# First two layers' down product as block products with fewer multiplications: five of eight pieces, weight sums on GpSimd, and four smaller edits

## The reference, cut to what matters

```python
# hybrid layer, l = 0 and 1
ada = cond_act @ w_ada + b_ada                      # 6 x 1024, also for the two layers of the second block
x = layer_norm(ALPHA * x + g1 * mixed) * ln1_g + ln1_b
u2 = layer_norm(x) * (1 + sc2) + sh2
hdn = jnp.square(jax.nn.relu(u2 @ w_up + b_up))     # 256 x 4096
x = layer_norm(ALPHA * x + g2 * (hdn @ w_down)) * ln2_g + ln2_b   # w_down 4096 x 1024

# attention layer of the second block
x1, x2 = jnp.split(x, 2, axis=-1)                   # rotary: halves of each head of 64
return x * cos + jnp.concatenate([-x2, x1], -1) * sin
# softmax of q.k for 8 difference maps and 8 window heads, over own and context keys
```

## Time and profile before

| | us |
|---|---|
| median of 3 runs | 2385.49 (2384.83 to 2390.07) |
| the profiled execution, its own time | 2385.63 |
| its span, first to last instruction | 2383.8 |
| PE busy in it | 2275.2 |
| DVE busy | 1006.3 |
| ACT busy | 346.3 |
| POOL busy | 69.9 |
| granted TensorE clock, mean | 0.994 |

### The profile page before, as it was taken

The page is one execution under the profiler, slowest core; times in us unless marked ns, Lnnn a source line. Parts: engine busy times, 40 slices in busy tenths (PEclk is TensorE's granted clock), DMA queues, the critical chain, the costliest instruction groups (busy, mean ns, idle before and its releaser), DMA issues.

```text
span 2383.8 us, 26007 instructions
## 1 busy us (share of the span) xinstructions
PE 2275.2 (95%) x10472; PEld 1384.4 (58%) x10472; DVE 1006.3 (42%) x2156; ACT 346.3 (15%) x705; POOL 69.9 (3%) x100
## 2 busy tenths in 40 slices
PE   6999999999999999999999999988899999998888
PEld 4888688448888786467554444333397544443333
DVE  4265656667656567213853211111235522211112
ACT  1221011001221110011441111111100011111111
POOL 0100000002000000000000000000030000000000
PEclk9999999999999999999999999999999999999999
DMA  9745967855377688542069999999964399999997
GB/s 325 254 165 195 342 235 285 323 212 212 126 280 262 238 317 312 198 147 75 35 252 356 423 420 424 423 423 422 410 234 159 121 367 422 423 423 424 421 422 295
DMA packets 184613, 703.44 MB, mean 295 GB/s; under 512 B 9648, under 2 KB 19120, under 8 KB 159152
## 3 DMA queue, kind: packets, MB, share of 16 engines
q1 hardware_dynamic: 180688, 691.76, 74.6%
q0 software_dynamic: 3808, 10.00, 1.3%
HBM read 696.45 MB, written 5.28 MB: 294 GB/s over the span
## 4 chain that ended last, share of the span: by engine, by line
PE 77%; SPq 11%; DMA 6%; DVE 3%; ACT 1%; issue 1%; DVEq 0%; ACTq 0%
PE banks L630 75%; DMA ring<-in_exp_w_up_dram 6%; SPq L2651 4%; SPq L2653 3%; SPq L2699 2%; SPq L2649 1%; DMA ring<-in_w_ada_dram 1%; DVE arena L2239 1%; PE banks L692 0%; DVE acc L1830 0%; PE banks L1211 0%; PE banks L1019 0%; DVE acc L1803 0%; ACT UT L1463 0%; PE banks L1106 0%
## 5 line engine op out<-in xcount | busy, mean ns | idle before, releaser
L630 PE MATMUL banks<-ring,arena 128*64 128x512 f32 (+2 forms) x2624 | 719.8, 589 | 32.5 <-DMA ring<-in_exp_w_up_dram 21.1
L630 PE MATMUL banks<-UT,ring 128*128 128x256 f32 (+1 forms) x3680 | 720.5, 355 | 8.5 <-ACT UT L1463 3.9
L630 PEld LDWEIGHTS banks<-UT,ring 128*128 128x128 f32 x3680 | 619.7, 192 | 82.7 <-issue 9.5
L630 PEld LDWEIGHTS banks<-ring,arena 128*64 128x64 f32 (+1 forms) x2624 | 288.5, 151 | 433.1 <-issue 390.9
L630 PE MATMUL banks<-arena 128*64 128x512 f32 (+5 forms) x1220 | 238.8, 493 | 9.1 <-DMA arena<-in_exp_w_up_dram 4.6
L2238 DVE TENSOR_TENSOR arena<-arena,banks 128x512 f32<-128x512 f32 x32 | 34.0, 1063 | 434.6 <-PE banks L630 434.6
L1830 DVE SCALAR_TENSOR_TENSOR acc<-ring,cact,acc 128x512 f32<-128x512 f32 x280 | 212.7, 760 | 9.9
L630 PEld LDWEIGHTS banks<-arena 128*64 128x64 f32 (+2 forms) x1220 | 99.3, 158 | 135.7 <-issue 120.7
L1627 ACT ACTIVATE arena<-banks 128x512 f32<-128x512 f32 (+1 forms) x96 | 65.3, 680 | 771.4 <-PE banks L630 732.2
L2246 DVE TENSOR_TENSOR arena<-banks,acc 128x512 f32<-128x512 f32 x32 | 22.1, 692 | 185.7 <-PE banks L630 185.7
L630 PE MATMUL banks<-ring,XN 128*128 128x512 f32 (+1 forms) x192 | 73.1, 540 | 2.8 <-DVE XN L2003 2.8
(11 more groups left out here) (268 smaller groups left out, 1707.0 us busy)
## 6 DMA issues: line engine op xcount, KB each, us to landing
ring<-in_exp_w_up_dram SPq DMA_DIRECT2D x40, 2048.0 KB, 25.2
ring<-in_exp_w_gate_dram SPq DMA_DIRECT2D x40, 2048.0 KB, 26.0
ring<-in_exp_w_down_dram SPq DMA_DIRECT2D x38, 2048.0 KB, 26.2
ring<-in_w_in_dram SPq DMA_DIRECT2D x26, 2048.0 KB, 13.7
ring<-in_mod_w_dram SPq DMA_DIRECT2D x24, 2048.0 KB, 9.0
ring<-in_w_ada_dram SPq DMA_DIRECT2D x20, 2048.0 KB, 8.1
ring<-in_w_up_dram SPq DMA_DIRECT2D x16, 2048.0 KB, 9.1
ring<-in_w_down_dram SPq DMA_DIRECT2D x16, 2048.0 KB, 9.0
```

The costliest lines, as they stand in the source:

```text
L630: return nc.tensor.matmul(o, lhs, rhs, start=start, stop=stop)
```

## The change

Five parts.

1. **Down product of pieces 0 to 4**, both layers: the 2x2 blocks (two tiles of tokens by two halves of the rows; two halves of the rows by two halves of the columns) are multiplied by Winograd's form of Strassen's scheme, seven block products of two matmuls each. VectorE forms the sums of hidden blocks (`hidden_sums`, four per piece), GpSimd those of weight blocks (`down_weight_sums`, four of 128x1024), into scratch of two sets. Products 1, 5, 6, 7 stay in banks of their own over the five pieces; VectorE combines them with the gate and adds them to the residual (`shared_products`) under pieces 5 to 7. Products 2, 3, 4 and pieces 5 to 7 are summed in banks as before. The norm rows are loaded behind piece 4.
2. **Folds** in pairs: one product of 32 columns for two modulation steps, one eviction of eight columns.
3. **Swaps**: the halves of the heads are swapped by ACT, four copies of 32 partitions, from the bank into `acc`; `perm2` and its products go; the rotations of the last two query groups move into the loop, behind pairs 2 and 4.
4. **Early scores**: the first pair's scores, maxima and exponents come between the last two query groups, behind `hidsum_ready`; the lambda product moves ahead of the query pieces.
5. The gate row's store and load are separate functions, with a weight set between them.

The diff, cut to its core:

```diff
@@ tensor: modulation
+            def modulation(until, turning=False, hold=None):
+                while summed[0] + 2 <= until:
+                    n = summed[0]
+                    names = [("ada",) + MOD_STEPS[n + i] for i in range(2)]
+                    bank = take(pe, names[0], None if turning else n // 2 % 2 if hold is None else hold)
+                    group_of[names[1]] = group_of[names[0]]
+                    pe.wait_ge(acc_ready, n + 2)
+                    finish(mm(bank[:, 0:32], C("fold"), folded[:, n // 2 % 2, :, :], True, True), names[0])
+                    summed[0] = n + 2
@@ tensor: block_one
+                down = {i: take(pe, part[i]) for i in (1, 5, 6, 2, 3, 4)}
                 pe.wait_ge(hid_ready, 16 * (l + 1))
+                def strassen_piece(j):
...
+                    product(1, upper(0), w[:, 0:2, 0:512])
+                    product(2, lower(0), w[:, 2:4, 0:512])
+                    pe.wait_ge(row_sums_ready, DOWN_BOTH * l + j + 1)
+                    product(3, s4, w[:, 2:4, 512:D])
+                    pe.wait_ge(weight_sums_ready, DOWN_BOTH * l + j + 1)
+                    product(5, s1, t1)
+                    product(6, s2, t2)
+                    if j == 0:
+                        down[7] = take(pe, part[7], 0)
+                    product(7, upper(1), w[:, 0:2, 512:D])
+                    product(4, lower(1), t4).then_inc(dn_read, 1)
...
                 for j in range(DOWN_BOTH):
-                    down_piece(j, (0, 1))
-                    beside("dn", l, j)
+                    strassen_piece(j)
+                    beside("dn", l, j, hold=1)
                 for j in range(DOWN_BOTH, 8):
                     down_piece(j, (0,))
+                down[5] = take(pe, names[3])
@@ tensor: attention_block (rope_pair and its four calls removed)
                 for j in range(2):
                     w = wview(("ain", 0, j))
                     for q in range(2):
                         pair_feature(("ain", j, q, 0), w, q * N, UT)
+                        if (j, q) == (1, 0):
+                            pe.wait_ge(hidsum_ready, 1)
+                            scores(two[0])
@@ scalar
+            def swap_halves(n, bank, width, scale=1.0):
+                if n >= 2:
+                    act.wait_ge(rope_ready, 4 + n - 1)
+                for b in range(4):
+                    there, here = slice(32 * b, 32 * b + 32), slice(32 * (b ^ 1), 32 * (b ^ 1) + 32)
+                    x = A(acc[there, n % 2, 0:width], bank[here, 0:width], ACT.Copy, scale=scale)
+                x.then_inc(halves_swapped, 1)
@@ vector
+            def hidden_sums(l, j):
+                if j >= 2:
+                    dve.wait_ge(dn_read, 7 * l + j - 1)
...
+                link(V.tensor_tensor(s1, a21, a22, ALU.add))
+                link(V.tensor_tensor(s2, s1, a11, ALU.subtract))
+                V.tensor_tensor(a21, a11, a21, ALU.subtract)
+                V.tensor_tensor(s4, a12, s2, ALU.subtract).then_inc(row_sums_ready, 1)
@@ vector: block_one
                     if i % 2:
                         beside("up", l, i // 2, flush="last" if i == 15 else None)
+                dve.wait_ge(hid_ready, 16 * (l + 1))
+                for j in range(2):
+                    hidden_sums(l, j)
                 wait_evicted(dve, ("ada", l, 11, "x"))
                 gate_turn(l, 1)
                 for j in range(6):
                     beside("dn", l, j, flush="last" if (l, j) == (1, 3) else None)
+                    if j + 2 < DOWN_BOTH:
+                        hidden_sums(l, j + 2)
+                    if j == DOWN_BOTH - 1:
+                        shared_products(l)
@@ vector: attention_block, in the loop over pairs
+                    if p in (2, 4):
+                        q = p // 2 - 1
+                        wait_evicted(dve, ("ain", 1, q, 0))
+                        rotate_swapped(5 + q, QK[:, 4 + 2 * q:6 + 2 * q, :])
@@ gpsimd
+            def down_weight_sums(l, j):
+                w = piece(pool, ("dn", l, j)).rearrange("p (k d) -> p k d", d=D)
+                if j == 0:
+                    pool.wait_ge(x_ready, 4 * l + 2)
+                if j == 1:
+                    filled(pool, ("up", l, 7, 1))
+                if j >= 2:
+                    pool.wait_ge(dn_read, 7 * l + j - 1)
...
+                link(G.tensor_tensor(t1, b12, b11, ALU.subtract))
+                link(G.tensor_tensor(t2, b22, t1, ALU.subtract))
+                G.tensor_tensor(t4, b21, t2, ALU.subtract)
+                G.tensor_tensor(b12, b22, b12, ALU.subtract).then_inc(weight_sums_ready, 1)
```

214 lines of the change are left out of this document (145 added, 69 removed).

## The result

The changed kernel takes 2409.02 us (median of 4 executions, 2408.28 to 2411.2), the kernel before 2386.1 in the same comparison: a ratio of 1.0097 [1.0085, 1.011], **22.9 us slower**. The direction was forecast (2397.3, +11.7), the size was not: the time lies just above 2409, the upper end of the range. The profiled execution took 2411.2 with a span of 2409.4, which is 25.6 us over the 2383.8 of before.

What follows compares the result with a forecast made beforehand. TensorE, busy 95% of the span, was taken to bound the kernel. Down products with waits +19.0, folds -2.8 and -3.5, attention -1 gave +11.7 on 2385.63: 2397.3 us, range 2373 to 2409 (forecast's own 2389 to 2409).

Steps and rivals of the forecast that it cites:

- Block products: Down stages, TensorE: two block products fewer in each of ten pieces, 0.863 us each, -17.3 us in all.
- First wait: First down piece, each layer: TensorE's third product waits for VectorE's row sums, 12.3 us late.
- the hold: Down stages: GpSimd's sums make VectorE's two-SBUF-input instructions wait; 6.2 us of each layer's first delay.
- slow restart: TensorE behind a long pause: runs at half clock for a while, +1.8 us for each such pause.
- The turn: Down stages: each GpSimd sum of 128x1024 adds 2.0 us to VectorE, bounds 0 and 2.4.
- B: Down stages: wide GpSimd sums don't hold VectorE, so the kernel gets faster, 2376.9 us; chance 0.22.
- C: Down stages: VectorE and GpSimd take short turns within an instruction, about the same time, 2388.5 us; chance 0.20.
- D: Down stages: VectorE gets the row sums out in time and all edits count, 2361.0 us; chance 0.03.
- Second wait: Later down pieces: TensorE waits again for row sums, 8.1 us a layer or nothing; half taken, 4.0.
- Folds: 48 modulation folds become 24 wider ones, -2.8 us; two waits before the second up piece's fold go, -3.5.
- Attention: Swapping products saved against a wait and slow clock at the early scores: net -1 us, bounds -4 and +2.
- A: The forecast: first down piece's waits grown by GpSimd's turns, 2389.3 to 2405.5 us by the second wait; chance 0.55.

Runs made afterwards that it cites:

- quarters: Changed kernel with each GpSimd weight sum cut into four instructions of 128x256: 2399.13 us, ratio 1.0062.
- rows_ahead_turns: Changed kernel with GpSimd's sums cut in four, row sums ahead of the modulation steps, GpSimd's second set after the last square: 2393.38 us, 1.0029.
- strassen_folds: Changed kernel with the attention block of the kernel before: 2406.94 us, ratio 1.0089.
- nostrassen: Changed kernel with the down products of the kernel before, its folds and attention edits kept: 2383.18 us, ratio 0.9987.
- the first chain: Kernel before with folds alone, then attention edits added, then block products added: 2375.83, 2383.18 and 2409.02 us.
- rows_first: Changed kernel with the row sums of the first two pieces ahead of the up stage's last modulation step: 2400.22 us, ratio 1.0062.
- the folds kernel: Kernel before with only the paired folds of the change: 2375.83 us, ratio 0.9958.
- best2: The combined kernel: changed kernel with weight sums of pieces 1 to 4 on VectorE, first scores last, and queues reordered: 2365.2 us, 0.9906.

## Why the forecast had the sign right and the size wrong

*Block products, -17.3.* Right: 103.05 us where nothing waits, from 111.6.

*First wait, 12.3 a layer, of it 6.1 without the hold.* Right. The third product came 433.13 - (418.35 + 3.45) = 11.3 us late in the first layer and 11.7 in the second, to which the 1.4 by which the held square delayed the start come as in the forecast's count: 12.8 and 13.1. Without the hold, counted alike, it came 6.2 and 6.5 late. Its make-up was a little other: GpSimd's set began when the last up product ended, as said, but the square was held by 1.4 us, not 0.8, and TensorE's first two products then took 6.61 us instead of 3.45, so that less of the delay shows as a wait. The slow restart behind this wait, put at 1.8, was 2.5 and 3.2 us (twelve records in 3.78 + 4.21 and in 3.78 + 4.88, for 1.88 + 3.60 at full speed).

*The turn, 2.0 of each instruction, from the alternation of the earlier trace rows.* Right: a row sum went from 0.42 to 2.45. The rule of the Trainium skill ("SBUF — State Buffer", "Who interferes with whom"), an exclusive lock for the whole instruction, is borne out, both ways: quarters took 0.83, and GpSimd's sets got longer by VectorE's turns. Rivals B and C fall with the same rows, and D with the order of the code, until that is changed.

*Second wait, 8.1 a layer or nothing, "I take half, 4.0".* **This is the first step that failed.** It came in full: 1.15 + 5.24 us and 1.8 of half clock, 8.2, and 1.52 + 4.86 and 2.2, 8.6. The reason given for "nothing" was that VectorE just keeps up at a slightly shorter turn. The forecast's own numbers don't give that: twelve turns shorter by 0.3 us take 3.6 off a wait of 5.6. And VectorE had no such margin: beside the sets its modulation sums took 13.3 us for 5.5, and row sums in another order moved most of the loss (rows_ahead_turns). A mean of two outcomes was put into a sum whose other terms are those of the likeliest case; with it in full the block products give +27.2, and +25.8 was measured (+31.1 over strassen_folds).

*Folds, -2.8 and -3.5.* The sign is right, the size 4.2 too small: -10.5. (48 folds of 0.14 less 24 of 0.17 are 2.6, not 2.8.) A fold that goes takes more with it than its 0.14 us. Two up pieces with their folds were 28.07 us apart and are 27.85 (373.45 to 401.30), which makes 24 x 0.22 = 5.3 for the first term, if all pairs are like these; the two waits of 1.75 (3.5) are gone. These make 8.8; the other 1.7 is within what the medians of two kernels scatter.

*Attention, -1.* **The second step that failed**, by 5 to 6 in the stage itself, which got 4.3 and 5.1 us longer, and by 8.4 over nostrassen (+7.4). The wait for the filter's operands was put at 4.1 and was 4.0, the slow restart at 1.8 and was 9.21 - 7.17 = 2.0. These were seen. What was not: another 0.9 us for lambda's exponential, whose bank the scores take. And the early scores brought nothing back: the next pair's scores need a bank of the first pair's, which VectorE gives back only behind the scaling of the last query group; that waits for ScalarE's swap, and the swap for the group's own product, which all of the above had made late (2.84). And the two rotations in the loop each put a wait ahead of a pair's scores (1.03 and 1.27), where before there had been none beyond the 1.19 that both kernels have. The upper bound of +2, both rotations on the path, left the bank waits out.

*Together.* Against the forecast of +11.7, by the medians of the first chain: block products +6.8, folds -4.2, attention +8.4; sum 11.0 of the 11.2 us missed. By the other chain, over strassen_folds, it is +12.1, -4.2 and +3.1. In both chains the folds' surplus hid 4.2 us of what the two failed steps missed; that the time came out so near the range is luck to that extent. The range was said to leave out the worst of attention on top of A; by its own numbers, 2405.5 + 3, it took that in. What went past it is, by the one chain, attention beyond its bound of +2, by the other the block products beyond theirs of +27.2.

## What to carry to other kernels

Work given to GpSimd beside a busy VectorE is not hidden work: count each of its two-input SBUF instructions as time of VectorE (here some 2.0 us for each of 128x1024), and compare it with what VectorE would need itself (1.22). Before a wait is put into an in-order queue, ask what is ready behind it: ahead of a ready product it cost 4.9 us and 2.0 of slow clock here, behind it that wait was gone. Ask too whose bank the moved work takes, and when that is given back. And where a term is "x or nothing", decide which case the forecast is and take its value; half of it is the time of neither.

## What the runs showed of the hardware

Instructions of VectorE and GpSimd with two SBUF inputs exclude each other whole: 128x256 sums on VectorE took 0.42 us alone, 0.83 beside GpSimd instructions of 128x256, 2.45 beside such of 128x1024. A chain of seven modulation sums took 5.48 us alone, 7.9 beside the narrow ones and 13.3 to 13.9 beside four of the wide; the longer GpSimd instruction is the costlier neighbour, since in nearly all rows the two alternate one for one. The prediction read the earlier trace rows as if only VectorE instructions with two SBUF inputs were held (though its order of time lets the scaling take a turn). The scaling at the head of a modulation step, with one SBUF input and a scalar for each partition, is held too (0.49 us alone). Its row beside the first set in the changed kernel; then, from rows_first, a transpose and a reduction, which are not held (0.71 and 0.69 us are their lengths alone), and the GpSimd sum beside them:

```profile
403.64 2.57 DVE L1882 TENSOR_SCALAR acc<-ring,cact 128x512 f32<-128x512 f32 x1
```

```profile
448.63 0.71 DVE L1845 STREAM_TRANSPOSE acc<-acc 128x512 f32<-128x512 f32 x1
449.37 0.69 DVE L1846 TENSOR_REDUCE folded<-acc 128x16 f32<-128x512 f32 x1
```

```profile
448.45 2.36 POOL L2730 TENSOR_TENSOR UT<-ring 128x1024 f32<-128x1024 f32 x1 [0.65 <-DMA ring<-in_w_down_dram]
```

The granted clock fell to the 1.2 GHz level behind short pauses. Stretches of the changed kernel (columns as above, clock third from last):

```profile
420.00:425.00 5.00, 4.96 (x7) 1.69 (x5) 4.93 (x3) 0.00 (x0) 4.92 (x3) 0.57 1.04 410
...
433.13:437.00 3.87, 3.87 (x5) 1.80 (x6) 3.70 (x9) 0.00 (x0) 1.92 (x4) 0.50 1.01 374
...
1152.00:1156.00 4.00, 4.00 (x13) 2.87 (x14) 1.63 (x5) 2.20 (x4) 0.00 (x0) 0.50 0.02 4
```

Ahead of the first stands the pause of 3.29 us, of the second that of 8.16, of the third that of 4.88. Behind pauses of 1.85 us at the same product, in the folds kernel and the combined one, the records ran at full speed (32 in 13.97 us, 12 in 5.39). Behind 3.29 us it was one or the other: 6.61 and 5.37 us for the eight records in the two layers of the changed kernel, 3.67 in the first of the one with the attention of before. Behind 2.38 and 2.35 us (GpSimd in quarters) it was 5.20 and 5.24. Here these slow records cost nothing: the third product waits for the row sums either way, and came 14.8 us after the first both behind 6.61 us of records and 8.16 of wait, and behind 3.67 and 11.10 (strassen_folds).

And the clock fell once without a pause. In layer 1, behind a run of small products (64 and 4 rows), the folds kernel ran 16 records of a 128x256 product in 6.55 us, and before, changed and most other kernels in 3.72. The clock of the folds kernel in that stretch:

```profile
610.00:612.00 2.00, 2.00 (x7) 1.55 (x6) 2.00 (x8) 0.00 (x0) 0.00 (x0) 0.50 1.05 393
```

This is the 3.3 us by which its layer 1 is longer than that of the kernel without block products, and strassen_folds (5.41) and best2 (4.96) have part of it. The work there is the same in all of them. One execution of each kernel was profiled, so whether this goes with the kernel or with the execution, and why, stays open.
